# Two layers of a hybrid streaming encoder on one core: the projection to decays and betas from the raw tokens, with root and shift applied to its sums

## The chip, the cores and the metric

The kernel runs on one core of a Trainium2 chip. The metric is the device time of one execution in microseconds (us). Engines: TensorE (PE; its weight loads are PEld), VectorE (DVE), ScalarE (ACT), GpSimd (POOL), SyncE (SP).

## What is computed

Input x has 512 tokens of 1024 channels in fp32. Each of the two layers is a SwiGLU feed-forward, a token mixing and a second feed-forward, each behind an RMS norm that is modulated by a condition. What matters here is the input of the mixing and one projection of it:

```python
def _rmsnorm(x, g):
    return x * rsqrt(mean(x * x, axis=-1) + NORM_EPS) * g
def _modulate(h, shift, scale):
    return h * (1.0 + scale) + shift

h = _modulate(_rmsnorm(x, mix_norm_g[l]), sh2, sc2)      # (512, 1024)
... b_a, b_b ... = _split_cols(h @ w_in, IN_SIZES)       # 4 columns each of 5640
beta = sigmoid(b)
g = -exp(a_log) * softplus(a + dt_bias)
```

b_a and b_b are the raw decays and betas of the four heads of the delta rule (mixer B). For token t and column n the projection is the sum over channels k of (x[t,k] * r[t] * s[k] + m[k]) * w[k,n], with r the inverse root of the norm, s the gain times (1 + scale), m the shift. It equals r[t] * sum(x[t,k] * s[k] * w[k,n]) + sum(m[k] * w[k,n]).

## The kernel before

**Layout.** Channels lie on the 128 partitions, in eight rows (k) of 512 tokens: tile x is [128, 8, 512]. The modulated rows are kept split in two parts, uh and ul, both fp32r, with uh + ul the fp32 value. Weights come in units of 128 output channels. A unit (L524 to L535) is 8 x 3 matmuls of 128x128 by 128x512, wh*uh, wh*ul and wl*uh, into one bank of PSUM. Its weights come by DMA into raw, ScalarE rounds them to wh (L1155), and VectorE forms wl = raw - wh (L1526). wh and wl have two buffers, so that the split of unit n+2 waits until TensorE has ended unit n.

**Order of the mixing.** Each engine has its own list of instructions, written out by hand, and semaphores (sig) hold them together. TensorE's list begins at L707 with units 0 to 13: q, k, v of mixer B (0 to 5), the output gate (6, 7), q, k, v of mixer C (8 to 13). Behind unit 5 stands the projection to decays and betas: 8 rows of weights ab_w, each 128x32 (8 columns used, the others are zero), multiplied with uh and ul read as fp32 (L731). Rows g and g+4 go to column group g (32 partitions of bank 6), so each group adds up two of the eight rows, and four groups lie side by side on the array. Behind unit 7 small matmuls (L740) transpose ab_T, the copy of bank 6, and add the four groups, with ident_q as the moving operand: the result is [token, t*8 + slot] in bank 6, columns 0 to 31. Behind unit 9 and each of the next three come the head sums for the L2 norm of q and k (head_sums, L691, L692), which wait for VectorE's sq_l (L1752).

**ScalarE's list** (L1300 on), for m = 0 to 13: rounds the weights of unit m+2 (ahead), copies the result of unit m out of PSUM (L1252), copies bank 6 to ab_T in m = 6 (L1302), and in m = 2 to 7 puts the convolution of row m-2 through SiLU (L1306). In m = 8 it computes the nonlinear functions of decays and betas (ab_nonlinear, from L1281 on).

**VectorE's list** (L1721 on), for m = 0 to 5: forms wl of unit m+4 (ahead), then the causal convolution of row m in four instructions (L1759 and three times L1762). m = 6 adds a mask to a bias table (L1766), m = 7 clears five tiles (L1770), evicts the transposed decays and betas to sc (L1774) and adds dt_bias (L1776). m = 8 on: wl of unit m+2, sq_l, and from m = 10 the reciprocals of the L2 norms (L1735).

The lines most needed:

```python
for i, v in enumerate((uh, ul, uh, ul)):          # L728, behind unit 5
    for g in range(4):
        k = g + 4 * (i // 2)
        mm = e.matmul(PS[32 * g:32 * g + 32, 6, :], ab_w[:, k, :], v[:, k, :].bitcast(F32),
                      start=i == 0, stop=i == 3, skip_group_check=True)
mm.then_inc(ab_mm.sem, 1)
```

Of the kernel before, what the change touches and what calls it, by code (L numbers as in the profile page):

```python
# [21 lines left out]
F32 = mybir.dt.float32  # L22
F32R = mybir.dt.float32r
ALU = mybir.AluOpType
ACT = mybir.ActivationFunctionType
AX = mybir.AxisListType

P = 128
# [4 lines left out]
KD = D_MODEL // P  # L33
TT = SEQ // P
# [52 lines left out]
def encoder_kernel(nc, a, out):  # L87
    ctx = ExitStack()
    with ctx:
# [3 lines left out]
        def place(name, shape, dt, at=None):  # L93
            size = 4 * int(np.prod(shape[1:]))
            size = (size + 31) // 32 * 32
            off = base[0] if at is None else at
            if at is None:
                base[0] += size
            return nc.alloc_sbuf_tensor_at(name, shape, dt, offset=off)
# [54 lines left out]
        ab_T = place("ab_T", [P, SEQ], F32)  # L154
        gb = place("gb", [P, 2 * 8 * CHUNK], F32)
        warm = place("warm", [P, 2], F32)
        gate_hold = place("gate_hold", [P, SEQ], F32)
        ssq = place("ssq", [P, SEQ], F32)
        sq = place("sq", [P, 2, SEQ], F32)
# [106 lines left out]
        ab_mm = sig("ab_mm", 1)  # L266
        ab_copied = sig("ab_copied", 1)
        ab_tr = sig("ab_tr", 1)
        gate_out = [sig(f"gate_out{j}", 16 * 12) for j in range(2)]
        gate_back = [sig(f"gate_back{j}", 16 * 3 * 4) for j in range(2)]  # L270
        conv_done = sig("conv_done", 6)
# [249 lines left out]
        def _(e):  # L521
# [162 lines left out]
            def mixing(l):  # L684
# [39 lines left out]
                for m in range(3, 9):  # L724
                    proj(m)
                    if m == 5:
                        e.wait_ge(layer_in.sem, layer_in.at(l, 80))
                        for i, v in enumerate((uh, ul, uh, ul)):  # L728
                            for g in range(4):
                                k = g + 4 * (i // 2)  # L730
                                mm = e.matmul(PS[32 * g:32 * g + 32, 6, :], ab_w[:, k, :], v[:, k, :].bitcast(F32),  # L731
                                              start=i == 0, stop=i == 3, skip_group_check=True)
                        mm.then_inc(ab_mm.sem, 1)
                    if m == 7:
                        e.wait_ge(tables_in.sem, 16 * 10)
                        e.wait_ge(ab_copied.sem, ab_copied.at(l, 1))
                        for t in range(TT):
                            for g in range(4):
                                c0 = t * P + 32 * g
                                mm = e.matmul(PS[32 * g:32 * g + 32, 6, 8 * t:8 * t + 8], ab_T[:, c0:c0 + 32],  # L740
                                              ident_q[:, 0:8], start=True, stop=True)
                        mm.then_inc(ab_tr.sem, 1)
                e.wait_ge(same_done.sem, 1)
                for i in range(4):
# [405 lines left out]
        def _(e):  # L1150
# [86 lines left out]
            def mixing(l):  # L1237
# [60 lines left out]
                for m in range(14):  # L1298
                    project(m, bp[:, m, :] if m < M_C else ct[m - M_C][:, :], m % 4)
                    if m == 6:  # L1300
                        e.wait_ge(ab_mm.sem, ab_mm.at(l, 1))
                        e.activation(ab_T[:, :], PS[:, 6, :], ACT.Copy).then_inc(ab_copied.sem, 1)  # L1302
                    if 2 <= m <= 7:

                        e.wait_ge(conv_done.sem, conv_done.at(l, m - 1))
                        e.activation(bp[:, m - 2, :], t_buf[:, m % 2, :], ACT.Silu).then_inc(conv_silu.sem, 1)  # L1306
                    if 8 <= m <= 11:
                        i = m - 8
                        e.wait_ge(conv_silu.sem, conv_silu.at(l, i + 1))
                        if i >= 2:  # L1310
                            e.wait_ge(l2_mm.sem, l2_mm.at(l, i - 1))
                        e.activation(sq_h[:, i % 2, :], bp[:, i, :], ACT.Square).then_inc(l2_hi.sem, 1)
                        e.activation(sq[:, i % 2, :], bp[:, i, :], ACT.Square).then_inc(l2_sq.sem, 1)
                    if 9 <= m <= 12:
                        i = m - 9
                        if i >= 2:
                            e.wait_ge(qk_done.sem, qk_done.at(l, i - 1))
                        e.wait_ge(l2_mm.sem, l2_mm.at(l, i + 1))
                        e.activation(h32[:, i % 2, :], PS[:, 4 + i % 2, :], ACT.Sqrt, bias=eps[:, 0:1])\
                            .then_inc(l2_root.sem, 1)  # L1320
                    if m == 8:
                        ab_nonlinear()
                    if m == 10:
                        e.wait_ge(rows_mm.sem, rows_mm.at(l, 1))
                        for r in (slice(0, 4), slice(32, 36)):
                            e.activation(ab_T[r, :], PS[r, 7, :], ACT.Copy).then_inc(rows_done.sem, 1)
# [193 lines left out]
        def _(e):  # L1520
# [165 lines left out]
            def mixing(l):  # L1686
# [36 lines left out]
                for m in range(14):  # L1723
                    if m == 9:
                        ab_decay()
                    if m == 11:
                        e.wait_ge(gc_mm.sem, gc_mm.at(l, 1))
                        e.tensor_copy(sc[:, 128:160], PS[:, 6, 32:64]).then_inc(ab_v.sem, 1)
                        e.wait_ge(ab_v.sem, ab_v.at(l, 5))
                        TTo(sc[:, 208:224], sc[:, 144:160], sc[:, 128:144], ALU.subtract).then_inc(ab_v.sem, 1)  # L1730
                    if m >= 10:

                        i = m - 10
                        e.wait_ge(l2_root.sem, l2_root.at(l, i + 1))
                        e.reciprocal(h32[:, i % 2, :], h32[:, i % 2, :]).then_inc(l2_inv.sem, 1)  # L1735
                        e.wait_ge(l2_inv.sem, l2_inv.at(l, i + 1))
                        STT(out=bp[:, i, :], in0=bp[:, i, :], scalar=HEAD ** -0.5 if i < 2 else 1.0,
                            in1=h32[:, i % 2, :], op0=ALU.mult, op1=ALU.mult).then_inc(qk_done.sem, 1)
                    if m == 13:
                        e.wait_ge(ab_v.sem, ab_v.at(l, 6))  # L1740
                        differences(0)
                    if m < 6:
                        ahead(MIX + m + 2)
                    elif m >= 8:
                        ahead(MIX + m)
                    if 8 <= m <= 11:
                        i = m - 8
                        e.wait_ge(l2_hi.sem, l2_hi.at(l, i + 1))
                        e.wait_ge(l2_sq.sem, l2_sq.at(l, i + 1))
                        if i >= 2:  # L1750
                            e.wait_ge(l2_mm.sem, l2_mm.at(l, i - 1))
                        TTo(sq_l[:, i % 2, :], sq[:, i % 2, :], sq_h[:, i % 2, :], ALU.subtract).then_inc(l2_lo.sem, 1)  # L1752
                    if m < 6:

                        e.wait_ge(in_done.sem, in_done.at(l, m + 1))
                        if m >= 2:
                            e.wait_ge(conv_silu.sem, conv_silu.at(l, m - 1))
                        y, v = t_buf[:, m % 2, :], bp[:, m, :]
                        TS(y, v, conv_w[:, m, 3:4], None, ALU.mult).then_inc(conv_step.sem, 1)  # L1759
                        for back in (1, 2, 3):  # L1760
                            e.wait_ge(conv_step.sem, conv_step.at(l, 3 * m + back))
                            STT(out=y[:, back:], in0=v[:, :SEQ - back], scalar=conv_w[:, m, 3 - back:4 - back],  # L1762
                                in1=y[:, back:], op0=ALU.mult, op1=ALU.add)\
                                .then_inc((conv_step if back < 3 else conv_done).sem, 1)
                    if m == 6:
                        TTo(a_bias[:, :, :], a_bias[:, :, :], a_mask[:, :].unsqueeze(1).broadcast_to([P, 4, 2 * P]),  # L1766
                            ALU.add).then_inc(bias_masked.sem, 1)
                    if m == 7:
                        for lv in range(1, LEVELS):
                            e.memset(Ym[lv][:, :, :], 0.0)  # L1770
                    if m == 7:

                        e.wait_ge(ab_tr.sem, ab_tr.at(l, 1))
                        e.tensor_copy(sc[:, 32:64], PS[:, 6, 0:32]).then_inc(ab_v.sem, 1)  # L1774
                        e.wait_ge(ab_v.sem, ab_v.at(l, 1))
                        TTo(by_t(64), sc[:, 32:64].rearrange("p (t s) -> p t s", t=TT)[:, :, 0:4],  # L1776
                            small[:, 0:4].unsqueeze(1).broadcast_to([P, TT, 4]), ALU.add).then_inc(ab_v.sem, 1)
# [479 lines left out]
```

## Time and profile before

| | |
|---|---|
| time of three runs | 2336.10, 2336.37, 2337.31 us; median 2336.37 |
| profiled execution | 2336.95 us; its span from first to last instruction 2335.3 us |
| mean granted clock of TensorE | 0.998 |
| busy: PE, DVE, ACT, POOL | 2307.1, 1278.6, 849.4, 113.7 us |
| mixing, units 5 to 9, layer 0 | some 426 to 458 us of the span |
| the same, layer 1 | some 1572 to 1604 us of the span |

How to read it: one execution is recorded by the hardware. Times in the rows are microseconds from the span's start, unless marked ns. Matmuls are pipelined: the next starts before the one ahead has ended, so distances between starts are what one costs. "x8" is a merged row of eight instructions.

### The profile page before, as it was taken

The numbers are of one execution on the slowest core, as the hardware profiler recorded it, in microseconds if no ns is written. First come the engines' busy times: TensorE is split into PE (matmuls) and PEld (weight loads), VectorE is DVE, ScalarE is ACT, GpSimd is POOL, SyncE is SP. The second block draws the span as 40 slices with busy tenths as digits, with TensorE's granted clock in tenths as the row PEclk, the third lists the DMA queues.
The fourth block names the chain that finished last, engine by engine and source line by source line (L and its number), as shares of the span: only waits on it lengthen the run. The fifth ranks groups of instructions, "written<-read, shape, count | busy, mean of one in ns | idle before, by whom it ended". The sixth has DMA issues, their size and how long they took to land.

```text
span 2335.3 us, 37104 instructions
## 1 busy us (share of the span) xinstructions
PE 2307.1 (99%) x14326; PEld 1874.5 (80%) x14326; DVE 1278.6 (55%) x1790; ACT 849.4 (36%) x1255; POOL 113.7 (5%) x220
## 2 busy tenths in 40 slices
PE   7999999999999999999999999999999999999998
PEld 6888888778777888888878888887777788888886
DVE  4554556685457664433465545667656576443334
ACT  5321234532455442223343222345225555331232
POOL 1000010020000000000000000001000000000000
PEclk9999999999999999999999999999999999999999
DMA  8564563343234344433245645624332352453231
GB/s 322 189 215 153 176 199 124 108 137 96 96 113 149 113 135 153 144 99 103 95 140 185 207 144 192 215 90 114 105 101 91 118 176 93 151 169 101 91 111 59
DMA packets 95154, 325.33 MB, mean 139 GB/s; under 512 B 12904, under 2 KB 13576, under 8 KB 94016
## 3 DMA queue, kind: packets, MB, share of 16 engines
q1 hardware_dynamic: 57456, 216.09, 28.0%
q0 software_dynamic: 23760, 82.48, 11.3%
q10 hardware_dynamic: 13824, 25.17, 3.1%
q8 instruction: 81, 1.33, 0.2%
q14 instruction: 33, 0.27, 0.0%
HBM read 306.34 MB, written 14.73 MB: 137 GB/s over the span
## 4 chain that ended last, share of the span: by engine, by line
PE 90%; DVE 5%; ACT 2%; DMA 1%; issue 1%; SPq 0%; ACTq 0%; DVEq 0%; POOL 0%; POOLq 0%
PE PS L531 80%; PE PS L1077 2%; PE PS L811 2%; DVE h L1735 1%; DMA ada<-in_ada_first_dram 1%; DVE wl L1526 1%; DVE t_buf L1762 0%; PE PS L1051 0%; ACT wh L1155 0%; PE PS L803 0%; PE PS L1094 0%; PE PS L731 0%; PE PS L1011 0%; DMA ada_raw<-in_ada_w_dram 0%; PE PS L1060 0%
## 5 line engine op out<-in xcount | busy, mean ns | idle before, releaser
L1526 DVE TENSOR_TENSOR wl<-raw,wh 128x1024 fp32r<-128x1024 f32 (+2 forms) x360 | 466.2, 1295 | 779.6 <-ACT wh L1155 778.8
L531 PE MATMUL PS<-uh,wh 128*128 128x512 f32 x2176 | 861.1, 396 | 2.4 <-DVE wl L1526 1.5
L531 PE MATMUL PS<-ul,wh 128*128 128x512 f32 x2176 | 848.0, 390 | 0.0
L531 PE MATMUL PS<-uh,wl 128*128 128x512 f32 x2176 | 847.8, 390 | 0.0
L1155 ACT ACTIVATE wh<-raw 128x1024 fp32r<-128x1024 f32 (+2 forms) x360 | 401.6, 1115 | 868.0 <-PE PS L531 851.6
L531 PEld LDWEIGHTS PS<-uh,wh 128*128 128x128 f32 x2176 | 408.3, 188 | 99.6 <-issue 5.9
L531 PEld LDWEIGHTS PS<-uh,wl 128*128 128x128 f32 x2176 | 408.5, 188 | 86.5
L531 PEld LDWEIGHTS PS<-ul,wh 128*128 128x128 f32 x2176 | 408.7, 188 | 80.6
L531 PE MATMUL PS<-hh,wh 128*128 128x512 f32 x736 | 287.0, 390 | 0.0
L531 PE MATMUL PS<-hl,wh 128*128 128x512 f32 x736 | 286.3, 389 | 0.0
L531 PE MATMUL PS<-hh,wl 128*128 128x512 f32 x736 | 286.3, 389 | 0.0
L1605 DVE SCALAR_TENSOR_TENSOR ada_raw<-ada_raw,cond 128x1024 f32<-128x1024 f32 x144 | 172.3, 1219 | 3.7 <-DMA ada_raw<-in_ada_w_dram 3.5
L531 PEld LDWEIGHTS PS<-hh,wl 128*128 128x128 f32 x736 | 138.2, 188 | 28.8
L531 PEld LDWEIGHTS PS<-hh,wh 128*128 128x128 f32 x736 | 138.2, 188 | 28.7
L531 PEld LDWEIGHTS PS<-hl,wh 128*128 128x128 f32 x736 | 138.2, 188 | 28.5
L473 POOL DMA_DIRECT2D ada_raw<-in_ada_w_dram x144 | 76.4, 531 | 1621.6 <-DVE ada_raw L1605 1619.4
L1215 ACT ACTIVATE hh<-h 128x512 f32 (+1 forms) x88 | 55.6, 632 | 173.8 <-DVE h L1647 170.9
L1651 DVE TENSOR_TENSOR hl<-h,hh 128x512 f32 (+1 forms) x88 | 60.9, 692 | 77.9 <-ACT hh L1215 77.9
L1627 DVE SCALAR_TENSOR_TENSOR x<-PS,gate_eff,x 128x512 f32<-128x512 f32 x80 | 59.7, 746 | 15.7 <-PE PS L531 15.7
L1164 ACT ACTIVATE sq<-x 128x512 f32<-128x512 f32 x49 | 31.0, 632 | 88.2 <-DVE x L1627 87.4
L1647 DVE TENSOR_TENSOR h<-silu_s,PS 128x512 f32<-128x512 f32 x85 | 57.8, 680 | 0.0
L1077 PE MATMUL PS<-oh,wh 128*128 128x512 f32 x128 | 50.0, 391 | 0.0
(280 smaller groups left out, 1624.1 us busy)
## 6 DMA issues: line engine op xcount, KB each, us to landing
raw<-in_ffn_in_dram SPq DMA_DIRECT2D x176, 512.0 KB, 3.6
ada_raw<-in_ada_w_dram POOLq DMA_DIRECT2D x144, 512.0 KB, 3.9
raw<-in_mix_in_dram SPq DMA_DIRECT2D x88, 512.0 KB, 3.6
raw<-in_ffn_out_dram SPq DMA_DIRECT2D x32, 768.0 KB, 4.4
raw<-in_ffn_out_dram SPq DMA_DIRECT2D x32, 640.0 KB, 3.9
g_in<-gates_dram ACTq DMA_DIRECT2D x48, 256.0 KB, 3.0
ada<-in_ada_first_dram SPq DMA_DIRECT2D x8, 1024.0 KB, 16.4
raw<-in_mix_up_dram SPq DMA_DIRECT2D x16, 512.0 KB, 3.7
```

Of the source, the lines that this page charges most:

```text
L473: e.dma_start(ada_raw[:, j, :], a["ada_w"][u]).then_inc(ada_in[j].sem, 16)
L531: mm = e.matmul(PS[:, bank, :], w[:, j % 2, k * P:(k + 1) * P], v[:, k, :], start=(k == 0 and w is wh and v is xh), stop=(k == K - 1 and w ...
L811: return e.matmul(PS[o, bank, ts * HALF:(ts + 1) * HALF].rearrange("p (b w) -> p b w", w=2 ** lv), lhs[r, ts, :], v, start=True, stop=True)
L1077: mm = e.matmul(PS[:, 3 * (d % 2) + b, :], w[:, d % 2, k * P:(k + 1) * P], v[:, k, :], start=(k == ks[0] and w is wh and v is oh), stop=(k ...
L1155: e.activation(wh[:, j % 2, 0:K * P], raw[:, j, 0:K * P], ACT.Copy).then_inc(hi_ready.sem, 1)
L1164: e.activation(ssq[:, :] if d == 0 else sq[:, d % 2, :], x[:, d, :], ACT.Square).then_inc(sq_done.sem, 1)
L1215: e.activation(dst, h32[:, j // 2, :], ACT.Copy).then_inc(hh_done.sem, 1)
L1526: TTo(wl[:, j % 2, 0:K * P], raw[:, j, 0:K * P], wh[:, j % 2, 0:K * P], ALU.subtract)\
L1605: STT(out=ada_raw[:, j, :], in0=ada_raw[:, j, :], scalar=1.0, in1=cond[:, :], op0=ALU.mult, op1=ALU.mult, accum_out=ada_sum[:, bass.ds(u, ...
L1627: STT(out=x[:, d, :], in0=PS[:, bank, :], scalar=gate_eff[:, d:d + 1], in1=x[:, d, :], op0=ALU.mult, op1=ALU.add).then_inc(x_done.sem, 1)
L1647: TTo(h32[:, j // 2, :], silu_s[:, j // 2, :], PS[:, 2 + j // 2, :], ALU.mult)\
L1651: TTo(hl[:, slot, :].rearrange("p a n -> p (a n)"), h32[:, j // 2, :], hh[:, slot, :].rearrange("p a n -> p (a n)"), ALU.subtract).then_in ...
```

## The change

The product of ab_w with the scale of the norm is formed on VectorE (ab_ws, in the space of gb, which is free then). TensorE multiplies ab_w with the shift (one column, into bank 4) and ab_ws with x itself. ScalarE also copies the shift's product; TensorE adds up its four groups beside the transposes. VectorE multiplies the transposed sums with the inverse root of each token and adds the shift's product.

```diff
+        ab_ws = gb[:, 0:KD * 32].rearrange("p (k n) -> p k n", k=KD)
...
...
                         e.wait_ge(layer_in.sem, layer_in.at(l, 80))
-                        for i, v in enumerate((uh, ul, uh, ul)):
+                        for i in range(2):
                             for g in range(4):
-                                k = g + 4 * (i // 2)
-                                mm = e.matmul(PS[32 * g:32 * g + 32, 6, :], ab_w[:, k, :], v[:, k, :].bitcast(F32),
-                                              start=i == 0, stop=i == 3, skip_group_check=True)
+                                k = g + 4 * i
+                                e.matmul(PS[32 * g:32 * g + 32, 4, 0:1], ab_w[:, k, :], mod[:, k:k + 1],
+                                         start=i == 0, stop=i == 1, skip_group_check=True)
+                        e.wait_ge(ab_scaled.sem, ab_scaled.at(l, 1))
+                        for i in range(2):
+                            for g in range(4):
+                                k = g + 4 * i
+                                mm = e.matmul(PS[32 * g:32 * g + 32, 6, :], ab_ws[:, k, :], x[:, k, :],
+                                              start=i == 0, stop=i == 1, skip_group_check=True)
                         mm.then_inc(ab_mm.sem, 1)
...
+                        for g in range(4):
+                            mm = e.matmul(PS[32 * g:32 * g + 32, 6, 64:72], warm[:, 1:2].broadcast_to([P, 32]),
+                                          ident_q[:, 0:8], start=True, stop=True)
                         mm.then_inc(ab_tr.sem, 1)
...
                         e.wait_ge(ab_mm.sem, ab_mm.at(l, 1))
+                        e.activation(warm[:, 1:2], PS[:, 4, 0:1], ACT.Copy)
                         e.activation(ab_T[:, :], PS[:, 6, :], ACT.Copy).then_inc(ab_copied.sem, 1)
...
+                    if m == 2:
+                        TTo(ab_ws, ab_w[:, :, :], scale_eff[:, :].unsqueeze(2).broadcast_to([P, KD, 32]), ALU.mult)\
+                            .then_inc(ab_scaled.sem, 1)
...
                         e.wait_ge(ab_tr.sem, ab_tr.at(l, 1))
-                        e.tensor_copy(sc[:, 32:64], PS[:, 6, 0:32]).then_inc(ab_v.sem, 1)
+                        e.wait_ge(rstd_done.sem, rstd_done.at(l, 2))
+                        by_row = lambda v: v.rearrange("p (t s) -> p t s", t=TT)
+                        TTo(by_row(sc[:, 32:64]), by_row(PS[:, 6, 0:32]), rstd_tok[:, :].unsqueeze(2).broadcast_to([P, TT, 8]),
+                            ALU.mult).then_inc(ab_rooted.sem, 1)
+                        e.wait_ge(ab_rooted.sem, ab_rooted.at(l, 1))
+                        TTo(by_row(sc[:, 32:64]), by_row(sc[:, 32:64]), PS[:, 6, 64:72].unsqueeze(1).broadcast_to([P, TT, 8]),
+                            ALU.add).then_inc(ab_v.sem, 1)
```

## Rows read from the trace of the kernel before

**Rows 1.** The page: busy time of the engines, chain that ended last by engine.

```profile
PE 2307.1 (99%) x14326; PEld 1874.5 (80%) x14326; DVE 1278.6 (55%) x1790; ACT 849.4 (36%) x1255; POOL 113.7 (5%) x220
...
PE 90%; DVE 5%; ACT 2%; DMA 1%; issue 1%; SPq 0%; ACTq 0%; DVEq 0%; POOL 0%; POOLq 0%
```

**Rows 2.** Timeline of TensorE around the block in layer 0: start us, us, engine, instruction.

```profile
431.85 1.07 PE L731 MATMUL PS<-uh,ab_w 128*32 128x512 f32 x8
...
434.44 1.04 PE L731 MATMUL PS<-ul,ab_w 128*32 128x512 f32 x8
435.42 0.50 PE L531 MATMUL PS<-uh,wh 128*128 128x512 f32 x1
```

**Rows 3.** Timeline of VectorE in the same stretch; in brackets idle before, and releaser.

```profile
431.44 2.32 DVE L1762 SCALAR_TENSOR_TENSOR t_buf<-bp,conv_w,t_buf 128x511 f32<-128x511 f32 x3
435.41 1.23 DVE L1526 TENSOR_TENSOR wl<-raw,wh 128x1024 fp32r<-128x1024 f32 x1 [1.64 <-ACT wh L1155]
```

**Rows 4.** Timelines of TensorE and VectorE in layer 1.

```profile
1577.93 1.07 PE L731 MATMUL PS<-uh,ab_w 128*32 128x512 f32 x8
...
1581.50 0.50 PE L531 MATMUL PS<-uh,wh 128*128 128x512 f32 x1
...
1577.40 2.32 DVE L1762 SCALAR_TENSOR_TENSOR t_buf<-bp,conv_w,t_buf 128x511 f32<-128x511 f32 x3
```

**Rows 5.** Timeline of TensorE, token sums of the norm.

```profile
398.13 0.43 PE L585 MATMUL PS<-ones_mean,ssq 128*32 128x1 f32 x32 [0.20 <-DVE ssq L1540]
```

**Rows 6.** Multiplies on VectorE: the tile sc (ns min/median/max), and the timeline.

```profile
L1711 DVE TENSOR_TENSOR lT<-gb,sc x4: 684/684/685, 486.5 to 1657.3; 128x512 f32<-128x512 f32 x4
...
459.57 0.17 DVE L1693 SCALAR_TENSOR_TENSOR sc<-sc 128x16 f32<-128x16 f32 x1 [1.79 <-ACT sc L1286]
459.78 0.17 DVE L1696 SCALAR_TENSOR_TENSOR sc<-sc 128x16 f32<-128x16 f32 x1
```

**Rows 7.** Timelines of VectorE and TensorE at the third head sums.

```profile
470.70 0.68 DVE L1752 TENSOR_TENSOR sq_l<-sq,sq_h 128x512 fp32r<-128x512 f32 x1
...
471.44 0.50 PE L691 MATMUL PS<-sq_h,same_r 128*128 128x512 f32 x1 [0.24 <-DVE sq_l L1752]
```

**Rows 8.** Timelines of ScalarE and VectorE behind the block, layer 0.

```profile
441.25 1.06 ACT L1155 ACTIVATE wh<-raw 128x1024 fp32r<-128x1024 f32 x1 [1.20 <-PE PS L531]
...
446.35 0.63 ACT L1306 ACTIVATE bp<-t_buf 128x512 f32<-128x512 f32 x1 [3.07 <-DVE t_buf L1762]
...
455.70 0.13 DVE L1774 COPY sc<-PS 128x32 f32<-128x32 f32 x1
455.87 0.17 DVE L1776 TENSOR_TENSOR sc<-sc,small 128x16 f32<-128x16 f32 x1
...
457.10 0.68 DVE L1752 TENSOR_TENSOR sq_l<-sq,sq_h 128x512 fp32r<-128x512 f32 x1
```

**Rows 9.** Timelines of TensorE and ScalarE, and engine time by window, around the first head sums.

```profile
457.92 0.42 PE L691 MATMUL PS<-sq_h,same_r 128*128 128x512 f32 x1
...
456.08 0.22 ACT L1281 ACTIVATE sc<-sc 128x16 f32<-128x16 f32 x1 [0.76 <-DVE sc L1776]
...
456.00:464.00 8.00, 8.00 (x38) 6.25 (x38) 3.71 (x7) 7.82 (x13) 0.00 (x0) 1.00 0.22 66
```

**Rows 10.** Timeline of TensorE, the transposes of ab_T.

```profile
446.52 0.44 PE L740 MATMUL PS<-ident_q,ab_T 128*32 128x8 f32 x32
```

**Rows 11.** Timeline of TensorE at the key products.

```profile
486.60 1.16 PE L785 MATMUL PS<-bp 64*64 64x64 f32 x64 [0.20 <-DVE bp L1737]
```

**Rows 12.** TensorE's two longest pauses inside its work, and the granted clock behind each (PEclk).

```profile
17.97 1.10 PE L546 MATMUL PS<-ada,cond_k 128*32 128x64 f32 x64 [2.39 <-DMA ada<-in_ada_first_dram]
...
36.82 0.30 PE L546 MATMUL PS<-ada,cond_k 128*32 128x64 f32 x4 [2.02 <-issue]
...
18.00:21.00 3.00, 1.74 (x66) 1.20 (x66) 1.83 (x9) 2.06 (x3) 0.00 (x0) 1.00 1.01 421
...
37.00:41.00 4.00, 4.00 (x70) 2.91 (x70) 1.89 (x8) 1.86 (x3) 2.13 (x4) 0.57 0.56 213
```

More of the change, by code:

```diff
@@ L268, in encoder_kernel @@
         ab_tr = sig("ab_tr", 1)
+        ab_scaled = sig("ab_scaled", 1)
+        ab_rooted = sig("ab_rooted", 1)
         gate_out = [sig(f"gate_out{j}", 16 * 12) for j in range(2)]
```

## The prediction

> **What bounds the kernel now.** I read the page first: TensorE is busy 99% of the span and is 90% of the chain that ended last [rows 1]. So a microsecond taken from its queue counts only as long as nothing else is late at the next place where it waits. Then I read the timeline around the lines that the diff touches, per engine. The projection to decays and betas (L731, after unit 5) runs on TensorE from 431.85 us; unit 6 starts behind it at 435.42 [rows 2]. It is 3.57 us of a queue that is full before and behind. Its 16 matmuls are 32 instructions, two for each; eight groups of four stand in it, four groups side by side on four column groups of the array. Six groups pass between the starts 431.85 and 434.44, so one group costs 0.43 us.
>
> What runs beside it matters more. VectorE ends the convolution of m=2 (four instructions, L1759 and L1762) at 431.44+2.32 = 433.76; ScalarE takes its result and then splits the weights of unit 7, and VectorE's next split starts at 435.41, after 1.64 us of idling [rows 3]. In layer 1 TensorE starts the block at 1577.93 and leaves it at 1581.50, and VectorE's convolution ends at 1577.40+2.32 = 1579.72 [rows 4].
>
> **The change, part by part.**
>
> *Removed.* Four of the eight groups: 4 x 0.43 = 1.72 us of TensorE per layer [rows 2]. The block before is 7 steps and a tail of 3.57 - 7 x 0.43 = 0.56; the block of four is 3 x 0.43 + 0.56 = 1.85 us. The operand is x in place of the split rows; both are read as fp32 in the same shape, and the cost of a group is taken as the same, from the same rows, at both ends.
>
> *The shift product* (8 matmuls with one column, 16 instructions) is added ahead of it. The nearest row is the token sums, 32 instructions on 32-wide tiles with one column in 0.43 us [rows 5], so 0.2 us, at most 0.43. It comes out at nothing, for it lies inside the wait that follows.
>
> *The wait for the scaled weights.* This decides. The product ab_w times scale stands on VectorE behind the convolution of m=2, in program order. TensorE comes to its wait at about 431.85+0.2 = 432.1, and VectorE is in the convolution until 433.76. The multiply is 128x256. Ends: 0.17 us for 16 columns and 0.68 us for 512 [rows 6]; on the line between them (0.51 us for 496 columns) 256 columns are 0.42 us, which I take. VectorE's instructions overlap by some 0.1 us where nothing is waited for, so it ends at about 434.09. TensorE starts 0.06 us behind such a release (sq_l ends at 471.38, the matmul starts at 471.44 [rows 7]): 434.15. The block then ends at 434.15+1.85 = 436.00 instead of 435.42: **0.58 us later**, though it has half of the work. Layer 1: multiply ends at 1580.05, released at 1580.11, unit 6 at 1581.96 instead of 1581.50: **0.46 us later**. With the ends 0.17 and 0.68 for the multiply this is 0.3 and 0.8, 0.2 and 0.7. VectorE itself pays nothing: the multiply fits in its idle 1.64 us [rows 3]. Behind the waiting instruction are units 6, 7 and all of TensorE's queue; for unit 6 waits the split of unit 8 on ScalarE, which before had idled 1.20 us for it [rows 8], so all that hangs on that split goes later by the same 0.58 (0.46).
>
> *What hangs on it.* From 441.25 the work is a serial chain of ScalarE and VectorE: split, convolutions, mask, memsets, and then the eviction of the decays at 455.70 with its sum at 455.87; behind it on VectorE are unit 10's split and sq_l at 457.10, ending at 457.78 [rows 8]. The first head sums of TensorE start at 457.92, only 0.14 us behind that end [rows 9].
>
> *The longer eviction* (L1774): one copy becomes a multiply by the roots, a wait, and an addition of the shift. Steps of that kind: 0.17 us from the copy to its follower [rows 8], 0.21 us between two dependent small ones [rows 6]. Two steps of 0.23 (32 columns instead of 16) less 0.17 are **0.29 us** in the serial chain, between 0.2 and 0.4. The wait for the roots is met long before (the reciprocal belongs to the norm). ScalarE cannot hide it: it already idles 0.76 us for this very eviction before 456.08, and is then busy 7.82 of the 8 us from 456 to 464 [rows 9]; TensorE's third head sums at 471.44 wait for sq_l of VectorE [rows 7]. So the chain from 455.70 to 471.44 takes the 0.58+0.29 = 0.87 whole.
>
> *The small copies.* One ScalarE copy of 128x1 before the copy to ab_T: nearest row 0.22 us for 128x16 [rows 9]; at nothing, since ScalarE then idles 3.07 us for VectorE before 446.35 [rows 8], and TensorE reads ab_T only at 446.52 [rows 10]. If that cover were gone it would be 0.2 us. Four matmuls (8 instructions) more after the transposes: 32 instructions take 0.44 us there [rows 10], so 0.11 us. They move TensorE to +0.69, less than VectorE's +0.87, so they cost nothing more. No DMA is added or moved, and the queues of SP and POOL are as they were, 0.87 us later.
>
> **Sum.** Layer 0: 0.58+0.29 = 0.87. Layer 1: 0.46+0.29 = 0.75, as ScalarE and VectorE stand there in the same order. At 486.60 TensorE again waits for VectorE (0.20 us) [rows 11], so nothing has been won back by then, and behind it TensorE is the one that is full. In all +1.62 us. Against the profiled execution: 2336.95+1.62 = 2338.57; that one was 0.58 above the median, so against the median 2336.37 it is **2338.0 us**. By bounds (0.17 to 0.68 twice, 0.2 to 0.4 twice) the sum is +0.9 to +2.4: 2337.3 to 2338.8.
>
> **Rivals.**
>
> *B, the weights are ready in time* (the multiply starts earlier than I read, or the wait is short). Then the block ends 1.72 us sooner. ScalarE could use only the 1.20 us that it idles at 441.25 [rows 8], so the chain goes -1.20+0.29 = -0.91 per layer, some -1.9 in all: 2334.4; if the chain does not hold TensorE either, -1.72+0.11 twice, -3.2: 2333.2. For it: TensorE is the bound on the page. Against it: the order of VectorE's instructions, and 433.76 against 432.1. Chance 0.12, of this 0.03 for the whole gain.
>
> *C, the clock falls in the new pause.* Mechanism: TensorE now idles from 432.1 to 434.15 and from 1578.1 to 1580.1. The one place in the trace where the granted clock fell is behind a pause of this size: 2.02 us until 36.82, then a mean clock of 0.57 from 37 to 41 us, most of it at the 1.2 GHz level; a pause of 2.39 us until 17.97 did not do it, the clock was 1.00 behind it [rows 12]. What it would cost: 4 us at 0.57 are 1.7 us of work, on top of 0.87. In one layer: 2339.7. In both: +1.62+3.44 = +5.1, **2341.4**, slower by 0.22%. It decides from the second layer on: one fall leaves the time within 0.2%. Chance 0.13 for one layer, 0.07 for both, since one of two such pauses did it, and ahead of ours the array is packed with 128x512 matmuls, without small gaps.
>
> The Trainium skill has such a rule (TensorE: Matmul & The Clock Gate, "The HAM clock gate"): the throttled state is the default and activity of the array releases it. By it a quiet stretch may give the half clock back. The trace agrees behind one pause and not behind the other.
>
> *A, the forecast:* 0.66. The rest, 0.02, is for a wait that no row of before shows.
>
> **How the numbers follow.** A measurement of this kernel can tell about 0.2% from no change, which is 4.7 us; the removed work as a whole is 3.4. So every case but C in both layers is within it. Faster by over 0.2%: 0.01. Slower: 0.07 for C in both, 0.01 for the rest: 0.08. Same: 0.91. The range reaches from B's 2334.4 to just past C in one layer, 2340.0; left out are C in both and B's whole gain, some 0.1, with a rest for the spread of runs.
>
> **What the profile after would show.** The block at L731's place has a pause of some 2 us between its one-column matmuls and the products with x, with VectorE's multiply as the releaser; four groups instead of eight; unit 6 begins at about 436.0 and 1582.8 (1581.96 and the 0.87 of layer 0); ScalarE's split at 441.8; the small sum of the decays some 0.9 us later; the head sums at 458.8 and 472.3 waiting for sq_l; the granted clock 1.00 behind the pause. It is wrong if the multiply starts before the convolution of m=2 has ended, if the pause is under a microsecond, or if the clock behind it is 0.5.

## The result, and the profile after

The changed kernel takes 2341.02 us (median of 15 runs, 2339.3 to 2344.72) against 2335.96 for the kernel before (15 runs, 2335.05 to 2337.74): ratio 1.0022, 95% interval 1.0015 to 1.0029. It is 5.1 us slower, just above the stated range. The profiled execution took 2341.02 us, span 2339.4.

The page of the changed kernel, the lines that answer to [rows 1]:

```profile
PE 2308.2 (99%) x14342; PEld 1877.0 (80%) x14342; DVE 1279.3 (55%) x1794; ACT 849.4 (36%) x1257; POOL 113.3 (5%) x220
```

TensorE's busy time is 1.1 us higher, though half of the block's work is gone. A matmul under a slower clock is busy for longer, and most of this is not at the block: the first 60 us have 1.4 us more (mean granted clock 0.94 instead of 0.97) and the end, from 3.5 us ahead of the last token sums, 1.0 us more (0.68 instead of 0.73). The mixing of layer 0, where the clock fell, has 0.4 us more, that of layer 1, where it did not, 1.1 us less.

The timeline of TensorE in the changed kernel, layer 0, answers to [rows 2]. L734 is the shift's product, L740 the products with x ("gb" is the place of the scaled weights), L534 is unit 6:

```profile
431.79 0.31 PE L734 MATMUL PS<-mod,ab_w 128*32 128x1 f32 x16
434.13 3.24 PE L740 MATMUL PS<-x,gb 128*32 128x512 f32 x16 [2.03 <-DVE gb L1779]
437.29 0.80 PE L534 MATMUL PS<-uh,wh 128*128 128x512 f32 x1
```

VectorE beside it, answering to [rows 3]:

```profile
431.41 2.32 DVE L1775 SCALAR_TENSOR_TENSOR t_buf<-bp,conv_w,t_buf 128x511 f32<-128x511 f32 x3
433.65 0.42 DVE L1779 TENSOR_TENSOR gb<-ab_w,scale_eff 128x256 f32<-128x256 f32 x1
435.38 1.23 DVE L1539 TENSOR_TENSOR wl<-raw,wh 128x1024 fp32r<-128x1024 f32 x1 [1.30 <-ACT wh L1167]
```

And the granted clock there (stretch, its length, busy PE, PEld, DVE, ACT, POOL, PEclk, DMA share, GB/s):

```profile
432.00:434.00 2.00, 0.09 (x12) 0.01 (x1) 1.93 (x4) 0.23 (x1) 0.00 (x0) 1.00 0.89 242
434.00:436.00 2.00, 1.87 (x12) 0.57 (x16) 0.70 (x2) 1.83 (x3) 0.00 (x0) 0.65 0.05 21
436.00:438.00 2.00, 2.00 (x10) 0.61 (x3) 1.93 (x4) 0.00 (x0) 0.00 (x0) 0.50 0.12 18
438.00:440.00 2.00, 2.00 (x10) 1.64 (x9) 1.32 (x2) 0.61 (x1) 0.00 (x0) 1.00 0.72 244
```

The pause is 2.03 us, VectorE's multiply releases it, and the products start at 434.13. Behind it the clock goes to 0.50 (the 1.2 GHz level) for some 3.4 us: the sixteen instructions take 3.24 us, and unit 6 begins at 437.29 instead of 435.42. In layer 1 the same pause is followed by no fall (the answer to [rows 4]):

```profile
1582.27 1.92 PE L740 MATMUL PS<-x,gb 128*32 128x512 f32 x16 [1.88 <-DVE gb L1779]
1584.12 0.50 PE L534 MATMUL PS<-uh,wh 128*128 128x512 f32 x1
...
1582.00:1584.00 2.00, 1.73 (x16) 0.42 (x16) 0.69 (x2) 1.97 (x3) 0.00 (x0) 1.00 0.11 43
```

Here the block lasts 1582.27 to 1584.12 = 1.85 us. Further on, TensorE waits for VectorE at the third head sums and at the key products as before [rows 7, 11], later by 2.4 us:

```profile
473.88 0.51 PE L694 MATMUL PS<-sq_h,same_r 128*128 128x512 f32 x1 [0.23 <-DVE sq_l L1765]
...
489.03 1.16 PE L797 MATMUL PS<-bp 64*64 64x64 f32 x64 [0.20 <-DVE bp L1750]
```

**One yardstick for all kernels.** The whole time of one execution spreads by some 4 us, but the part that the edits touch does not. I take from each trace the time from the token sums that open the mixing (L585, for instance 398.13 in [rows 5]) to the start of the key products (486.60 in [rows 11]): 88.47 us in layer 0 of the kernel before. It contains the block and the whole serial chain.

| kernel | layer 0 | layer 1 | median of all runs; before beside it |
|---|---|---|---|
| before (first trace) | 88.47 | 88.48 | 2335.96 |
| before_again | 88.47 | 88.47 | 2336.66; 2336.27 |
| changed (first trace) | **90.94** | 89.25 | 2341.02; 2335.96 |
| after_again | 89.32 | **90.91** | 2340.39; 2336.27 |
| third_look | 89.28 | 89.29 | 2340.13; 2336.63 |
| filled_eight | 89.28 | 89.37 | 2338.15; 2336.63 |
| filled_pause | 89.51 | 89.60 | 2340.07; 2336.42 |
| shorter_pause | 88.50 | 88.47 | 2336.54; 2336.27 |
| pause_in_before | 90.53 | 90.39 | 2341.59; 2336.42 |
| early_scale | 87.40 | 87.26 | 2335.76; 2336.42 |
| one_copy | 87.18 | 87.04 | 2334.30; 2336.63 |
| block_behind_6 | 87.37 | 87.25 | 2337.55; 2336.42 |
| before_memsets_later | 87.74 | 87.71 | 2335.27; 2336.63 |
| memsets_later | 86.21 | 86.22 | 2332.42; 2336.27 |

Bold: the granted clock fell behind the pause. Traces of one kernel without a fall agree within 0.07 us, and a fall adds 1.62 us (90.91 - 89.29).

### The profile page after: what moved, and what is told of

It is laid out like the page before. It is cut to its first block, busy times and chain, and to the rows that moved or that the text cites. A ratio compares the mean times of both kernels' runs of the same rounds, so it can differ in the third digit from the quotient of the medians.

```text
span 2339.4 us, 37144 instructions
## 1 busy us (share of the span) xinstructions
PE 2308.2 (99%) x14342; PEld 1877.0 (80%) x14342; DVE 1279.3 (55%) x1794; ACT 849.4 (36%) x1257; POOL 113.3 (5%) x220
## 4 chain that ended last, share of the span: by engine, by line
PE 87%; DVE 7%; ACT 2%; issue 2%; DMA 1%; SPq 0%; ACTq 0%; DVEq 0%; POOL 0%; POOLq 0%
PE PS L534 78%; PE PS L1089 2%; PE PS L823 2%; DVE h L1748 1%; DVE wl L1539 1%; DVE t_buf L1775 1%; ACT wh L1167 1%; DVE t_buf L1589 0%; DVE ul L1596 0%; DMA ada<-in_ada_first_dram 0%; PE PS L1063 0%; PE PS L815 0%; PE PS L1106 0%; PE PS L1023 0%; PE PS L1072 0%
## 5 line engine op out<-in xcount | busy, mean ns | idle before, releaser
L534 PE MATMUL PS<-uh,wh 128*128 128x512 f32 x2176 | 861.1, 396 | 2.3 <-DVE wl L1539 1.3
L534 PE MATMUL PS<-ul,wh 128*128 128x512 f32 x2176 | 848.0, 390 | 0.0
L534 PE MATMUL PS<-uh,wl 128*128 128x512 f32 x2176 | 847.8, 390 | 0.0
L534 PEld LDWEIGHTS PS<-uh,wh 128*128 128x128 f32 x2176 | 408.4, 188 | 99.0 <-issue 5.6
L534 PEld LDWEIGHTS PS<-uh,wl 128*128 128x128 f32 x2176 | 408.5, 188 | 86.7
L534 PEld LDWEIGHTS PS<-ul,wh 128*128 128x128 f32 x2176 | 408.8, 188 | 81.1
L534 PE MATMUL PS<-hh,wh 128*128 128x512 f32 x736 | 287.0, 390 | 0.0
L534 PE MATMUL PS<-hl,wh 128*128 128x512 f32 x736 | 286.4, 389 | 0.0
L534 PE MATMUL PS<-hh,wl 128*128 128x512 f32 x736 | 286.3, 389 | 0.0
L534 PEld LDWEIGHTS PS<-hh,wl 128*128 128x128 f32 x736 | 138.1, 188 | 28.7
L534 PEld LDWEIGHTS PS<-hl,wh 128*128 128x128 f32 x736 | 138.2, 188 | 28.7
L534 PEld LDWEIGHTS PS<-hh,wh 128*128 128x128 f32 x736 | 138.1, 188 | 28.6
```

Of the source, the lines that this page charges most:

```text
L534: mm = e.matmul(PS[:, bank, :], w[:, j % 2, k * P:(k + 1) * P], v[:, k, :], start=(k == 0 and w is wh and v is xh), stop=(k == K - 1 and w ...
```

## The experiments

**The pause taken away: early_scale.**

```diff
-                    if m == 2:
+                    if m == 1:
                         TTo(ab_ws, ab_w[:, :, :], scale_eff[:, :].unsqueeze(2).broadcast_to([P, KD, 32]), ALU.mult)\
```

> The changed kernel with one move: VectorE forms the scaled weights behind the convolution of m=1 instead of m=2, 5.6 us earlier, in an idle gap of 1.65 us. Theory 1 (the pause before the products with x, and the clock that falls behind it, make the loss): no pause, clock 1.00 at the block, unit 6 begins some 1.7 us sooner than in the kernel before; ScalarE's split of unit 8 gains its 1.2 us of idling, the longer eviction takes 0.29 back, so about -0.9 us per layer, near 2334 us against 2336. Theory 2 (the longer eviction and the added small instructions make the loss, the clock fell by chance): the time stays near 2341. Theory 3 (the products with x from the new weights' place are slower than those with the split rows): the block of four groups takes clearly over 1.85 us at clock 1.00, and the time stays above 2336.

Measured: 2335.76 against 2336.42, ratio 0.9996 (0.9987 to 1.0005). The timeline of TensorE and the clock in early_scale:

```profile
431.78 0.31 PE L734 MATMUL PS<-mod,ab_w 128*32 128x1 f32 x16
431.93 1.90 PE L740 MATMUL PS<-x,gb 128*32 128x512 f32 x16
433.76 0.50 PE L534 MATMUL PS<-uh,wh 128*128 128x512 f32 x1
...
430.00:434.00 4.00, 4.00 (x42) 1.98 (x41) 3.62 (x5) 0.43 (x2) 0.00 (x0) 1.00 0.46 123
```

There is no pause, and the block starts at 431.93 and is left at 433.76: 1.83 us. That is no more than four groups should take, so theory 3 falls. The yardstick is 1.07 and 1.22 us below the kernel before (expected 0.9), and the changed kernel's loss is gone, so theory 2 falls too. The median shows 0.7 of these 2.3 us; where the rest went stands below.

**The pause without the work's change: pause_in_before.**

```diff
                         e.wait_ge(layer_in.sem, layer_in.at(l, 80))
+                        e.wait_ge(conv_done.sem, conv_done.at(l, 3))
                         for i, v in enumerate((uh, ul, uh, ul)):
```

> The kernel before with one wait added: TensorE waits ahead of the block for the end of the convolution of m=2, with all eight groups of work and nothing else changed. The block starts at 433.8 instead of 431.85. Theory 1: 2.0 us of pause and 1.7 us of clock per layer, with both layers +4 without the clock and +7.4 with it: near 2343. Theory 2: +4 at most, 2340. If a later idle stretch of ScalarE and VectorE took the pause up: near 2336.

Measured: 2341.59 against 2336.42, ratio 1.0023 (1.0013 to 1.0032). The pauses are 1.99 and 1.85 us, and the yardstick grows by 2.06 and 1.92: nothing behind takes a pause up. In the one trace the clock did not fall at either, and that execution, 2339.2, was the shortest of ten. The two pauses are 4.0 us by the yardstick, and the median is 5.2 us above the kernel before: what the other 1.2 us are, the trace does not show.

**The pause filled: filled_pause and filled_eight.** The second corrects the first, whose nine matmuls ended after the release.

```diff
+                        for i in range(8):          # 9 in filled_pause
+                            e.matmul(PS[:, 5, :], uh[:, 0, 0:P], uh[:, i % KD, :], start=True, stop=True)
                         e.wait_ge(ab_scaled.sem, ab_scaled.at(l, 1))
```

> The changed kernel with nine matmuls of 128x128 by 128x512 (9 x 0.227 = 2.04 us) put into the pause, between the shift's products and the wait for the scaled weights; their result in bank 5 is not used. TensorE's queue is not shortened and VectorE's release comes at the same time. Theory 1: the clock stays at 1.00, unit 6 begins at about 436.0 instead of 437.3, and the whole is what the forecast had without the clock, +1.6 us: near 2337.6. If the clock is no part of it: as the changed kernel, near 2341.

> filled_pause with eight matmuls instead of nine, since nine reached some 0.2 to 0.3 us past the release of the scaled weights. Theory 1: no fall of the clock at the block; the mixings last as the changed kernel's without its falls, about 420.5 and 420.0 us; time below the changed kernel's by what the falls cost it. If they fall in half of the pauses, 1.7 us less (near 2339); if in nearly all, 3.4 less (near 2337.5).

Measured: filled_pause 2340.07 against 2336.42 (1.0014, 1.0005 to 1.0024), filled_eight 2338.15 against 2336.63 (1.0007, 0.9998 to 1.0016). The timeline and the clock in filled_eight, whose mixing opens 1.5 us later than in the first traces:

```profile
433.31 0.31 PE L734 MATMUL PS<-mod,ab_w 128*32 128x1 f32 x16
433.54 2.11 PE L737 MATMUL PS<-uh 128*128 128x512 f32 x8
435.63 1.93 PE L742 MATMUL PS<-x,gb 128*32 128x512 f32 x16
...
434.00:436.00 2.00, 2.00 (x12) 1.17 (x14) 1.54 (x3) 0.73 (x2) 0.00 (x0) 1.00 0.65 246
436.00:438.00 2.00, 2.00 (x18) 0.73 (x11) 1.12 (x1) 1.34 (x2) 0.00 (x0) 1.00 0.00 0
```

The yardstick, 89.28 and 89.37, is the changed kernel's where its clock did not fall, to 0.1 us. So the products start when they did, and within the mixings only the clock can differ. The median is 2.0 to 2.9 us below those of the changed kernel (2340.13 to 2341.02), its 11 runs lie within 2336.9 and 2339.8, and +1.5 us against before is near the sum that the forecast had without the clock. Taken alone, that would put 2 to 3 us of the loss on the clock.

filled_pause speaks against taking it alone. Its pauses are filled as well, its trace has no fall between the first 45 us and the end, and by the yardstick it is only 0.23 us per layer longer than filled_eight. Yet its median is 1.9 us above filled_eight's, 2.5 above the 2337.6 that theory 1 expected, and hardly below the changed kernel's. Neither trace has a fall in the mixings or between them, so some 1.5 us of this difference is not explained, and medians can't tell the clock's share to better than that. And four filled pauses without a fall prove little when most open ones have none either: six of eight, as the next runs and pause_in_before show.

**The changed kernel again: after_again and third_look** (no edit), and the kernel before again.

> The changed kernel, once more. Without a fall of the clock a mixing should last 419.58+0.94 and 419.11+0.93 us, with one 1.7 us more. Theory 1: the clock falls behind at least one of the two pauses; median near 2341 again. If the clock fell by chance in the first trace: no fall, and a median near 2338.

> The changed kernel, for a third trace and the share of pauses with a fall: so far one of two in each of two traces. Theory 1: at least one fall again, a median near 2341. If falls are rarer than one in two, none in this trace.

> The kernel before, once more, for its own spread and a second trace. By stages between the token sums of the norms the first trace had 398.1 us to the first mixing, 419.6 and 419.1 us for the two mixings, 11.9 us for the tail. Theory 1 (the loss lies in the mixings): the mixings repeat within 0.1 us, whatever the other stages do. If the stages outside the mixings differ by 1 to 3 us between two executions of one kernel, such differences between kernels are no effect of an edit.

Measured: ratios 1.0018 (1.0009 to 1.0028), 1.0018 (1.0009 to 1.0027) and 1.0 (0.9991 to 1.0009). The rows of after_again, layer 1, and its clock:

```profile
1579.98 3.62 PE L740 MATMUL PS<-x,gb 128*32 128x512 f32 x16 [1.86 <-DVE gb L1779]
1583.53 0.50 PE L534 MATMUL PS<-uh,wh 128*128 128x512 f32 x1
...
1580.00:1582.00 2.00, 2.00 (x12) 0.61 (x16) 0.76 (x1) 1.69 (x3) 0.00 (x0) 0.51 0.01 2
```

Now it is layer 1 that falls, and the block takes 3.55 us instead of 1.85. In third_look neither did, and that execution, 2336.25, is the second shortest of its 11. So my expectation of a fall in each trace failed: it is two of six pauses in three traces. All three traced executions lie at or below the median of their runs, so traces may show fewer falls than the median execution has; the share itself stays open. Falls at the block are also not what mainly spreads the executions: the traced ones of third_look (2336.25) and filled_eight (2339.8, the longest of its 11) have no fall there and the same yardstick, and differ by 3.6 us, of which 2.6 lie ahead of the first mixing (it opens at 396.97 and 399.60).

**The pause shortened: shorter_pause.**

```diff
+                            if m == 2 and back == 2:
+                                TTo(ab_ws, ab_w[:, :, :], scale_eff[:, :].unsqueeze(2).broadcast_to([P, KD, 32]),
+                                    ALU.mult).then_inc(ab_scaled.sem, 1)
...
-                    if m == 2:
-                        TTo(ab_ws, ab_w[:, :, :], scale_eff[:, :].unsqueeze(2).broadcast_to([P, KD, 32]), ALU.mult)\
-                            .then_inc(ab_scaled.sem, 1)
```

> The changed kernel with the multiply of the scaled weights ahead of the last instruction of the convolution of m=2, 0.75 us earlier. The pause becomes 1.3 us instead of 2.0, the block ends 0.17 us sooner than in the kernel before, the longer eviction costs 0.29: +0.1 to +0.3 per layer without the clock. Theory 1, if any pause over a microsecond lets the clock fall: +1.7 per fall more, near 2340. If the clock needs the 2 us: near 2337.

Measured: 2336.54 against 2336.27, ratio 1.0001 (0.9992 to 1.001). TensorE's row in layer 0 of shorter_pause:

```profile
432.24 1.92 PE L740 MATMUL PS<-x,gb 128*32 128x512 f32 x16 [1.23 <-DVE gb L1779]
```

A pause of 1.23 us (1.10 in layer 1), no fall, and the yardstick back at 88.50 and 88.47. Moving one instruction ahead by 0.75 us takes some 4 us off the changed kernel. By the yardstick 0.8 of it per layer is the shorter wait; that the rest, some 2 us, goes with the falls is argued and not shown.

**Elsewhere on TensorE: block_behind_6.** The block stands behind unit 6 (`if m == 6:`), all else as changed.

> The changed kernel with the projection moved behind unit 6 on TensorE, where the scaled weights have long been ready; all else as changed. Theory 1: no pause, clock 1.00. Unit 6 ends 3.6 us sooner than before (437.6), unit 8's split on ScalarE starts at 440.0 instead of 441.25; the block of 1.85 us stands behind unit 6; the longer eviction takes 0.29: about -0.9 per layer, near 2334, as with the early scale. Theory 2: near 2341.

Measured: 2337.55 against 2336.42, ratio 1.0005 (0.9996 to 1.0014), which misses the 2334. The yardstick has what was expected, -1.10 and -1.22. The trace gives two places outside it where this execution lost: the first mixing opens at 399.56 instead of 398.13 (the start of the kernel, where all traces differ by up to 2.6 us), and at the entry of a loop in the first feed-forward of layer 1 TensorE waits 2.58 us, before 1.06. Together they are 2.9 us, so two kernels can lie this far apart for reasons outside the block.

**The longer eviction priced: one_copy.** early_scale with the old `e.tensor_copy(sc[:, 32:64], PS[:, 6, 0:32])`; root and shift are left out of the decays and betas, so the kernel serves only to price them.

> early_scale with the old single copy for the eviction of the decays: root and shift are left out of the decays and betas. It prices the longer eviction in the serial chain: forecast 0.29 us per layer; in early_scale's trace the copy and the addition behind it lie 0.38 us apart instead of 0.17, which is 0.21. So the third head sums about 0.2 us sooner than in early_scale in each layer, the mixings about 418.0 and 418.8 us. If the chain does not bind: no difference.

Measured: the yardstick is 0.22 us shorter than early_scale's in both layers, so this is what the two additional steps cost in the chain. The median, 2334.30 against 2336.63, ratio 0.9989 (0.998 to 0.9998), is 2.3 us below the kernel before where early_scale's was 0.7 below; 0.44 of that difference is the eviction, the rest lies outside the yardstick.

**The serial chain loosened: memsets_later and before_memsets_later.** The first is early_scale with this edit, the second the kernel before with it.

```diff
-                    if m == 7:
-                        for lv in range(1, LEVELS):
-                            e.memset(Ym[lv][:, :, :], 0.0)
...
+                    if m == 8:                      # behind sq_l
+                        for lv in range(1, 4):
+                            e.memset(Ym[lv][:, :, :], 0.0)
...
                     if m == 9:
                         ab_decay()
+                        for lv in range(4, LEVELS):
+                            e.memset(Ym[lv][:, :, :], 0.0)
```

> As early_scale, and the five memsets of VectorE (2.65 us) that stand ahead of the eviction of the decays in m=7 are moved behind sq_l in m=8 and behind the decays in m=9, into idle stretches. Forecast's claim that the serial chain of ScalarE and VectorE holds TensorE: then the head sums wait no longer, and a mixing lasts 1.5 us less than before in layer 0 and in layer 1 (418.1 and 417.6), near 2333. If TensorE is held by something else: as early_scale.

> The kernel before with the memsets moved as in memsets_later, and nothing else. It tells how much of that kernel's 4 us is the change's and how much the memsets'. If the change's removed 1.72 us per layer is the gain once the chain has slack: this kernel at 2335.5 to 2336, 0.2 to 0.4 per layer won from the waits of the head sums, and memsets_later 3.3 us below it. If the memsets are the gain: near 2332.5.

Measured: memsets_later 2332.42 against 2336.27, ratio **0.9983 (0.9974 to 0.9992)**, the version that beats both kernels. before_memsets_later 2335.27 against 2336.63, 0.9993 (0.9984 to 1.0002). VectorE's eviction in early_scale:

```profile
451.81 2.65 DVE L1786 MEMSET Ym<- 128x512 f32 x5
454.37 0.13 DVE L1792 TENSOR_TENSOR sc<-PS,rstd_tok 128x32 f32<-128x32 f32 x1
```

and in memsets_later, with the third head sums of TensorE behind it:

```profile
451.66 0.18 DVE L1794 TENSOR_TENSOR sc<-PS,rstd_tok 128x32 f32<-128x32 f32 x1
...
454.63 1.56 DVE L1770 MEMSET Ym<- 128x512 f32 x3
...
469.55 0.40 PE L694 MATMUL PS<-sq_h,same_r 128*128 128x512 f32 x1
```

The eviction comes 2.7 us sooner, and the third head sums no longer carry a wait. By the yardstick the memsets alone win 0.73 and 0.77 us per layer (0.2 to 0.4 was expected), and the change on top of them 1.53 and 1.49: 1.7 less the small instructions. So the removed matmuls are worth what the forecast said, as soon as neither the weights nor the chain are late.

## Why the forecast was wrong

By its own steps:

- *The removed work and the block of four:* 1.85 us forecast, 1.83 to 1.85 measured. Right. That x costs no more than the split rows: right.
- *The wait:* multiply 0.42 forecast and measured, release at 434.15 forecast, 434.13 measured. Without a fall unit 6 would have begun 0.5 to 0.6 us late: third_look has its unit 6 at 37.88 us behind the token sums in layer 0, the kernel before at 37.29, so 0.59 against the 0.58 of the forecast; layer 1 has 37.75 against 37.31, so 0.44 against 0.46. Right.
- *The longer eviction:* 0.29 forecast, 0.22 measured. *That all of it passes on:* 0.87 and 0.75 forecast, 0.81 and 0.82 measured at the key products (third_look). Right, and pause_in_before shows it for a pause alone.
- *The ends of the range and the chance of C:* this step failed. The forecast said that one pause of two had let the clock fall, and then gave 0.13 to a fall in one layer and 0.07 to falls in both, "since ... ahead of ours the array is packed with 128x512 matmuls". Nothing in the rows stood behind that discount; two of the six pauses in the three traces of the changed kernel had a fall (0.33 each, where the forecast's chances come to about 0.14), and C in both layers, whose time of 2341.4 is the nearest to what was measured, was left out of the range. Without the discount, one in two for each of the two pauses, one fall would have had half of the chance and both a quarter, a likeliest time of 2339.7, and a range that reaches over 2341.4. The price of a fall (1.7) was right: 1.62. The forecast also called the fall at 37 us the only one in the trace of the kernel before. There is one more at its end, where TensorE has pauses of 1.14 and 0.61 us and then little to do (stretch as above):

```profile
2320.00:2336.00 16.00, 5.43 (x88) 4.21 (x86) 6.28 (x10) 0.89 (x2) 0.00 (x0) 0.73 0.35 131
```

- *The missing term:* in layer 1, some 290 us into the mixing, TensorE stands still for 0.5 to 0.7 us, ended by nothing that the profile shows. The waits of TensorE in the changed kernel, from 300 to 2000 us (total, times, longest):

```profile
PE PS L740 <- DVE gb L1779: 3.9, 2, 2.0
...
PE PS L1063 <- issue: 0.5, 1, 0.5
```

It is there in all ten traces of kernels with the changed instructions and in none of the four with the old. No step of the forecast had it, and I have not found its cause.

The parts add up to 0.81+0.82+0.5 = 2.1 us without a fall, 3.8 with one, 5.4 with two; the first trace, with one in layer 0 and, at its end, a slower spread of the roots (2.08 us against 1.16, a fall that came there earlier than in the kernel before), has a span 4.1 us longer. The medians, +5.1, +4.1 and +3.5, would need 1.9, 1.2 and 0.9 falls per execution, where the traces have 0.7 on average, worth 1.1 us. So theory 1 is shown for the pause: early_scale and shorter_pause take it away and the loss with it, pause_in_before brings it into the other kernel. For the clock it is shown in two traces, at 1.62 us a fall. That falls make up the whole of what the medians have above 2.1 us is argued; 0.3 to 1.9 us of it stays open, and filled_pause and block_behind_6, with no pause at the block, stand 0.9 and 3.0 us above their own parts (the yardstick's difference and 0.5).

*What the median did not show of early_scale and block_behind_6.* At the entry of the loop in the first feed-forward of layer 1 TensorE waits for a split of VectorE, which itself stands behind a multiply that waits for a DMA of ada_raw. That wait was 1.1 and 2.1 us in the two traces of the kernel before, 2.2, 2.6 and 3.1 in early_scale, block_behind_6 and memsets_later, and 0 to 1.2 in the others. It can itself be the pause that lets the clock fall, as in before_again:

```profile
1216.27 0.58 PE L531 MATMUL PS<-uh,wh 128*128 128x512 f32 x1 [2.08 <-DVE wl L1526]
1216.65 0.63 PE L531 MATMUL PS<-ul,wh 128*128 128x512 f32 x1
...
1216.00:1220.00 4.00, 3.73 (x9) 2.94 (x10) 3.09 (x5) 0.63 (x1) 0.26 (x1) 0.57 0.77 246
```

Whether an earlier first mixing makes that wait longer, or these are differences between executions, was not tried.

## What to carry to other kernels

When work is taken off the engine that bounds a kernel and its operand now comes from another engine, look first at the producer's place in its own list: here a multiply of 0.42 us stood behind a convolution and made a pause of 2 us, and moving it by one step or less gave the whole loss back. A pause in a full TensorE queue has two prices, its length and the clock that may fall behind it (1.6 us here), and the second belongs in the sum with the share that the trace shows, not with a smaller one that no row supports. And judge such a change by a distance within the trace that repeats to hundredths; the whole time of an execution here spreads by several microseconds.

## What the runs showed of the hardware that was not expected

Of twelve pauses of TensorE between 1.85 and 3.1 us in an otherwise full queue (eight at the block, in four traces, and four at the loop's entry), four were followed by a fall of the granted clock to 0.5: those of 2.03, 1.86, 2.08 and 3.1 us; pauses of 1.85, 1.88, 1.99, 2.00, 2.03, 2.2 and 2.6 us were not. None of nine between 0.87 and 1.23 us was. Left out of the count are the first 45 us and the last 15 us of each trace, where the queue is not full and every trace has falls. So the clock falls behind the same pause of the same kernel in one execution and not in the next. The Trainium skill (TensorE: Matmul & The Clock Gate, "The HAM clock gate") calls the throttled state the default, which activity releases. The traces agree in so far as the clock was back at 0.5 behind four of these pauses, and show besides that the length of a pause alone does not decide it.
